# A two-layer encoder in one kernel: the projection by seven products in another order, a fourth raw weight buffer, two input sums on another engine, and both entries rearranged

## The reference

```
hn  = RMSNorm(h)
qkv = hn @ w_qkv                      (1024 x 2304)
h  += concat(attention A, attention B) @ w_o
h  += ConvGatedMLP(RMSNorm(h))        (1024 -> 5632 -> conv, SiLU gate -> 1024)
h  += (p[i] @ w_ple_proj) * sigmoid(RMSNorm(h) @ w_ple_gate)
```

## Time and profile before

| what | value |
|---|---|
| time, median of 3 runs | 2502.76 us (2502.4 to 2505.92) |
| the profiled execution's own time | 2506.71 us |
| its span | 2504.9 us |
| mean granted clock of TensorE | 0.992 |
| TensorE busy | 2433.6 us, 97% |
| VectorE busy | 1521.4 us, 61% |
| ScalarE busy | 1293.0 us, 52% |
| GpSimd busy | 1212.2 us, 48% |
| DMA, mean | 105 GB/s |

### The profile page before, as it was taken

How to read it: one execution, slowest core, us unless ns; L and a number is a source line. 1 busy time by engine, 2 the same in 40 slices (tenths; PEclk the granted TensorE clock), 3 DMA queues, 4 the chain that set the end, 5 groups by cost and what they waited for, 6 DMA issues and landing times.

```text
span 2504.9 us, 36613 instructions
## 1 busy us (share of the span) xinstructions
PE 2433.6 (97%) x12704; PEld 2116.9 (85%) x12704; DVE 1521.4 (61%) x2114; ACT 1293.0 (52%) x2020; POOL 1212.2 (48%) x881
## 2 busy tenths in 40 slices
PE   7998999999999999999989999999999999999999
PEld 6998998878888888888889889988788888888887
DVE  3587664276656668873255866733856656778733
ACT  5445774375555554444364467734655655533342
POOL 4877641148878860001339775412578888400011
PEclk9999999999999999999989999999999999999999
DMA  6642010313233248431226410103143233473312
GB/s 221 176 130 74 20 30 26 118 51 109 86 119 109 80 170 297 134 110 43 77 72 181 132 55 25 29 26 126 35 125 109 80 120 115 173 277 120 98 49 84
DMA packets 214060, 263.54 MB, mean 105 GB/s; under 512 B 17648, under 2 KB 145056, under 8 KB 213936
## 3 DMA queue, kind: packets, MB, share of 16 engines
q1 hardware_dynamic: 213376, 259.50, 32.9%
q0 software_dynamic: 560, 2.41, 0.3%
HBM read 206.83 MB, written 55.36 MB: 105 GB/s over the span
## 4 chain that ended last, share of the span: by engine, by line
PE 77%; DVE 7%; issue 6%; POOL 4%; ACT 4%; DMA 1%; SPq 0%; ACTq 0%; POOLq 0%; DVEq 0%
PE ps L3031 9%; PE ps L3034 9%; PE ps L3033 9%; PE ps L2554 7%; PE ps L2556 7%; PE ps L2555 7%; PE ps L3055 6%; PE ps L3056 6%; PE ps L3057 5%; PE ps L2807 3%; POOL w_hl L1051 2%; PE ps L2796 2%; PE ps L2725 1%; PE ps L2768 1%; PE ps L2900 1%
## 5 line engine op out<-in xcount | busy, mean ns | idle before, releaser
L1026 POOL TENSOR_TENSOR w_hl<-w_raw,w_hl 128x1024 fp32r<-128x1024 f32 x36 | 86.1, 2393 | 763.3 <-ACT w_hl L1247 763.3
L2554 PE MATMUL ps<-w_hl,xv 128*128 128x384 f32 x672 | 233.2, 347 | 28.7 <-POOL w_hl L1051 16.2
L2555 PE MATMUL ps<-w_hl,xv 128*128 128x384 f32 x672 | 228.8, 341 | 0.0
L2556 PE MATMUL ps<-w_hl,xv 128*128 128x384 f32 x672 | 228.6, 340 | 0.0
L2554 PE MATMUL ps<-w_hl,xT 128*128 128x512 f32 x512 | 202.0, 394 | 1.4 <-DVE xT L1900 0.7
L2556 PE MATMUL ps<-w_hl,xT 128*128 128x512 f32 x512 | 199.6, 390 | 0.0
L2555 PE MATMUL ps<-w_hl,xT 128*128 128x512 f32 x512 | 199.3, 389 | 0.0
L2384 DVE SCALAR_TENSOR_TENSOR ps<-c_up,ccols,ps 128x1023 f32<-128x1023 f32 x84 | 107.8, 1284 | 142.4 <-ACT ps L1679 142.4
L2363 DVE TENSOR_TENSOR c_up<-ps,kept 128x512 f32<-128x512 f32 x126 | 86.6, 689 | 125.2 <-ACT kept L1638 69.5
L2554 PEld LDWEIGHTS ps<-w_hl,xv 128*128 128x128 f32 x672 | 129.3, 192 | 36.1 <-POOL w_hl L1051 22.0
L3055 PE MATMUL ps<-bd_two,ad 128*128 128x512 f32 x392 | 152.5, 389 | 0.0
(11 more groups left out here) (322 smaller groups left out, 7309.8 us busy)
## 6 DMA issues: line engine op xcount, KB each, us to landing
ad_raw<-v_rows SPq DMA_DIRECT2D x70, 512.0 KB, 3.7
raw_a<-in_w_up SPq DMA_DIRECT2D x44, 512.0 KB, 5.0
raw_g<-in_w_up SPq DMA_DIRECT2D x44, 512.0 KB, 5.2
v_rows<-c_up SPq DMA_DIRECT2D x22, 1024.0 KB, 4.4
w_raw<-in_w_qkv SPq DMA_DIRECT2D x56, 384.0 KB, 3.3
w_raw_b<-in_w_qkv SPq DMA_DIRECT2D x48, 384.0 KB, 3.6
wd_main<-in_w_down SPq DMA_DIRECT2D x30, 512.0 KB, 8.2
v_rows<-hc_g SPq DMA_DIRECT2D x22, 512.0 KB, 5.0
```

The lines of the kernel that those rows point to most:

```text
L2554: nc.tensor.matmul(dst, lhs[:, k, 0, cols], wh, start=first, stop=False)
L2555: nc.tensor.matmul(dst, lhs[:, k, 0, cols], wl, start=False, stop=False)
L2556: return nc.tensor.matmul(dst, lhs[:, k, 1, cols], wh, start=False, stop=last)
```

## The change

The order of the products becomes 3, 5, 1, 4, 2, 7, 6. The ring of raw blocks gets a fourth buffer, `w_raw_d`, in the part of `w_hl`'s memory that the projection does not use; the projection's weights in `w_hl` are therefore packed. The two input sums on GpSimd are those of product 7 (i = 10 and 11, behind slots 26 and 30) and no longer of product 6; the weight sum for slot 32 stands behind the low part of slot 31. VectorE makes the low part of an input at m%3 = 0 between the second and the third add. At the entry ScalarE squares five token tiles and VectorE three; the high part of slot 3 stands ahead of the root, that of slot 4 between the first writes of the two output blocks; in layer 0 the first weight load stands ahead of the rows, and the loads of slots 2 to 6 ahead of the constants; waits for the constants move out of the entry. In layer 1 two of the first four slices are transposed behind rows 4 and 5 of the gate's last part, and their high and low parts stand behind the gate's last two tiles on ScalarE and VectorE. The bias set-up on GpSimd moves behind slots 7, 8, 9 and 11. At attention's entry the fills come one row earlier, the copies of the second head pair no longer wait for the second part of the head norms, and the four high parts stand ahead of the second root.

```diff
-Q_ORDER = (3, 5, 7, 4, 1, 2, 6)
+Q_ORDER = (3, 5, 1, 4, 2, 7, 6)
-Q_FINAL = {5: "C12", 1: "C11", 2: "C21", 6: "C22"}
+Q_FINAL = {5: "C12", 2: "C21", 7: "C11", 6: "C22"}
+Q_POOL = (10, 11)
+Q_LEAD = 2
-ENTRY_FILLS = {1: (0, 1), 2: (2,), 3: (3,)}
+ENTRY_FILLS = {0: (0, 1), 1: (2,), 2: (3,)}
+ONE_RING = 4
+SQUARED_FIRST = 5
...
         def one_raw(slot):
-            return w_raw_c[:, :] if slot % 3 == 2 else w_raw[:, slot % 3, 0:2 * QC]
+            at = slot % ONE_RING
+            if at == 3:
+                return w_raw_d[:, :, 4 * QC:5 * QC]
+            return (w_raw_c[:, :] if at == 2 else w_raw[:, at, 0:2 * QC]).rearrange("p (k n) -> p k n", k=2)
...
-                sp.wait_ge(s_w_low_ready, L * SLOTS + (slot + 1 if slot < 2 else slot))
+                if slot < 2:
+                    sp.wait_ge(s_w_low_ready, L * SLOTS + slot + 1)
+                elif slot == 3:
+                    sp.wait_ge(s_w_used, L * SLOTS + C_USED)
+                elif slot > 3:
+                    sp.wait_ge(s_w_low_ready, L * SLOTS + slot - 1)
...
+            load_qkv(0, 0)
             for j in range(TT // 2):
                 sp.dma_start(h[:, 2 * j:2 * j + 2, :], x_rows[:, 2 * j:2 * j + 2, :]).then_inc(h_loaded[j], 16)
-                if j < 2:
-                    load_qkv(0, j)
+                if j == 1:
+                    load_qkv(0, 1)
+            for slot in range(2, 7):
+                load_qkv(0, slot)
...
-                between = {1: set_consts, 2: negate_bias, 3: store_bias, 4: skew_bias} if L == 0 else {}
+                between = {7: set_consts, 8: negate_bias, 9: store_bias, 11: skew_bias} if L == 0 else {}
...
-                    if slot in (O0 - 10, O0 - 6):
-                        input_sum(12 if slot == O0 - 10 else 13)
-                    if slot + 2 < O0:
-                        qkv_sum(slot + 2)
+                    if slot == 26:
+                        input_sum(Q_POOL[0])
+                    if slot == 30:
+                        input_sum(Q_POOL[1])
+                        continue
+                    if slot == 31:
+                        qkv_sum(30 + Q_LEAD)
+                    if slot + Q_LEAD < O0:
+                        qkv_sum(slot + Q_LEAD)
...
                     pool.wait_ge(s_fill_ready, L * FILLS + (4 * hd + C_FILL - 4))
-                    if hd == 1:
-                        pool.wait_ge(s_q_rstd_ready, L * 2 + 2)
...
                     copies(hd)
-                    if hd == 0:
+                    if hd == 1:
                         low(O0)
+                        pool.wait_ge(s_q_rstd_ready, L * 2 + 2)
...
-                for m in range(4):
-                    first_high(m)
+                for m in range(2 if L else 0, 4):
+                    first_high(L, m)
...
                 first_keep(12)
+                square_tile(3)
                 first_keep(14)
-                square_tile(3)
+                square_tile(4)
                 if L:
                     table(ACT.Sqrt)
+                qkv_high(L, 3)
                 norm_root(0)
-                act.wait_ge(s_consts_loaded, CONSTS)
-                act.wait_ge(s_consts_set, 1)
...
                     for name, sign in Q_FIRST.get(q_product(m), ()):
+                        if m == 0 and name == "C22":
+                            qkv_high(L, 4)
...
-                entry_high(0)
-                entry_high(1)
+                act.wait_ge(s_consts_set, 1)
+                for f in range(4):
+                    entry_high(f)
                 act.wait_ge(s_q_mean_ready, L * 2 + 2)
                 nc.scalar.activation(q_rstd[:, :, 24:], q_sum[:, :, 24:], ACT.Sqrt).then_inc(s_q_rms_ready, 1)
-                entry_high(2)
-                entry_high(3)
...
+                        if n and t >= 6 and L < DEPTH - 1:
+                            first_high(L + 1, t - 6)
...
-                first_low(0)
-                first_low(1)
-                first_low(2)
-                first_low(3)
+                for m in range(2 if L else 0, 4):
+                    first_low(L, m)
                 first_keep(1)
                 first_keep(3)
+                square_tile(5)
                 first_keep(5)
                 first_keep(7)
-                square_tile(4)
+                square_tile(6)
                 first_keep(9)
-                square_tile(5)
                 first_keep(11)
-                square_tile(6)
+                square_tile(7)
                 first_keep(13)
-                square_tile(7)
                 first_keep(15)
...
-                    step_adds(m - 1)
-                    i = 2 * (m // 3 + 1)
-                    made = i < 14 and Q_ORDER[i // 2] in Q_INPUTS and Q_ORDER[i // 2] != 6
-                    if m % 3 == 0 and m > 1:
+                    if m % 3 == 0:
+                        step_adds(m - 1, (0, 1))
                         input_low(2 * (m // 3) + 1)
+                        step_adds(m - 1, (2, 3))
+                    else:
+                        step_adds(m - 1)
...
-                dve.wait_ge(s_w_used, L * SLOTS + (O0 - 1 + C_USED))
+                dve.wait_ge(s_w_sum, L * Q_TWO + Q_TWO)
                 for b in range(2):
                     nc.vector.memset(bias[0:HD, b, WIN_B - HD:WIN_B], BIG)
...
+                        if n and t >= 6 and L < DEPTH - 1:
+                            first_low(L + 1, t - 6)
...
+                    else:
+                        pe.wait_ge(s_gate_sig, L * 2 * TT - TT + 4)
+                        first_slice(L, 2)
+                        first_slice(L, 3)
...
+                        def next_slice(t):
+                            if t in (4, 5) and L < DEPTH - 1:
+                                pe.wait_ge(s_gate_sig, L * 2 * TT + (TT + t - 4 + 1))
+                                pe.wait_ge(s_gate_added, L * 2 * TT + (TT + C_GATE))
+                                first_slice(L + 1, t - 4)
```

More of the change, by code:

```diff
@@ L142, in q_squares, with one_bytes @@
     return 4 * sum(q_normed(x) for x in range(m))
+def one_bytes(L, s):
+    per = RAW_DMAS if s % ONE_RING < 2 else 16 * len(range(s % ONE_RING, O0, ONE_RING))
+    return L * per + 16 * (s // ONE_RING + 1)
 def q_twos(s):
@@ L157, in input_sums, with ring_free @@
 def input_sums(i):
-    return sum(Q_ORDER[x // 2] in Q_INPUTS and Q_ORDER[x // 2] != 6 for x in range(i))
+    return sum(Q_ORDER[x // 2] in Q_INPUTS and x not in Q_POOL for x in range(2, i))
+def ring_free(i):
+    return 6 * ((i - 3) // 2) + 4 + (i - 3) % 2 + 1
 def products_of(u):
@@ L318, in trunk @@
         r0 = ExitStack()
+        w_raw_d = sb("w_raw_d", [P, 2, 2048], F, r0)
+        r0.close()
+        r0 = ExitStack()
         bd_two = sb("bd_two", [P, 2, 2, 2, HALF], R, r0)
@@ L837, in tiled @@
                     return src.rearrange("a (k p) n -> p (a k) n", p=P)
-                for slot in range(0 if L else 2, O0):
+                for slot in range(0 if L else 7, O0):
                     load_qkv(L, slot)
@@ L2008, in step_adds @@
                         dve.wait_ge(s_q_copied, L * Q_COPIES + q_copies(m - 2))
-                    for t in range(4 if targets else 0):
+                    for t in tiles if targets else ():
                         q_add(m, 0, t)
@@ L2037, in _ @@
                         step_rest(m - 1)
[L2038 removed]
+                    if made and m % 3 == 2:
+                        input_sum(i)
+                    if i and m % 3 == 1:
                         input_low(i)
[L2040 to L2041 removed]
                     if m == QSTEPS - 2:
@@ L2544, in _, with first_slice @@
             pe.wait_ge(s_first_loaded, 32)
+            def first_slice(L, m, tiles=range(4)):
+                k, half = BY_TOKENS[m]
+                for t in tiles:
+                    last = nc.tensor.transpose(first_bank(m)[:, t * P:(t + 1) * P],
+                                               h[:, 4 * half + t, k * P:(k + 1) * P], ident[:, :])
+                if tiles[-1] == 3:
+                    last.then_inc(s_xfill, 1)
             for L in range(DEPTH):
```

199 lines of the change are left out of this document (101 added, 98 removed).

## The result

| | before | changed |
|---|---|---|
| median of 20 runs each, side by side | 2504.76 us | 2498.18 us |
| lowest to highest | 2500.61 to 2507.14 | 2495.42 to 2504.21 |
| ratio to before, 95% interval | | 0.9976 (0.9969 to 0.9982) |
| profiled execution, own time | 2506.71 us | 2496.61 us |
| its span | 2504.9 us | 2494.8 us |

The change is a gain, but a third of the one forecast (2484, range 2473 to 2497), and the time lies above the range. The two profiles differ by 10.1 us and not by 6.6: the one of before lies high among its runs, the one of the changed kernel low. I use them for where time went, stretch by stretch, and the medians for how much.

What follows compares the result with a forecast made beforehand. TensorE, busy 97% of the span, was taken as the bound, so only its waits and low clock could be won. Terms -5.9 - 4.1 - 4.2 - 2.6 - 1.8 - 1.3 + 0.8 = -19.1 from 2506.7, less 3.95: 2484 us, range 2473 to 2497.

Steps and rivals of the forecast that it cites:

- Entry: Slots 2 to 5: earlier high parts shrink stalls and low clock, gaining 5.9 us in layer 0, 4.1 in layer 1.
- The lock: Port pair shared by VectorE and GpSimd: held exclusively for a whole instruction, so delays are whole instructions.
- Layer 1's slot 3: Entry of layer 1: stall shrinks from 3.07 to about 1.6 us, with no fall of the clock.
- The skew transfer: Slots 10 to 13, layer 0: the transfer moved to slot 11 delays a weight load, +0.8 us, bounds 0 and +5.
- Slots 24 and 25: VectorE's low part no longer beside a GpSimd sum and behind two adds, not four: -4.2 and -2.6 us.
- Slots 30 to 37: Products with most adds parted, product 7's input sums on GpSimd: -0.9 us each layer, -1.8 together.
- Attention's entry: Second `k_nat` no longer waits for the second root: -0.4 and -0.85 us, together -1.3, bounds -5.3 and +2.7.
- d: Attention's entry: delay of VectorE's work before the first scores, beside GpSimd's earlier copies; taken as 2 us, from 0 to 4.
- Start of the projections: Start of both layers' projections: zero change; bound -1.9 us in layer 1.
- Given back: Rival, 0.20: clock falls at layer 1's entry, port delays attention's entry by 4 each layer, slots 30 to 37 unchanged; 2492.6 us.
- GpSimd becomes the bound: Rival, 0.05: steps with two weight blocks slow when VectorE blocks GpSimd operations, 1.1 us over in each of 24; 2510 us.
- signs of being wrong: TensorE stall above 2 us for GpSimd in slots 12-23 or 34-41, late raw load near slot 13, entry excess above 3 us.

Runs made afterwards that it cites:

- Experiment 4: Changed kernel, but GpSimd's weight sum for slot 5 waits until VectorE has refined the norm factors; 2493.25 us, ratio 0.9955.
- experiment 5: Changed kernel with bias set-up behind slots 4 to 7, sinks' copies moved, entry reordered on ScalarE and GpSimd, layer 1's table load earlier; 2480.31 us, 0.9912.
- experiment 7: Changed kernel, but VectorE's low part of an input at the third step stands behind all four adds, as before; 2503.4 us, 0.9996.
- experiment 1: Changed kernel, but bias set-up with its skew transfer behind slots 4, 5, 6, 7 of layer 0, not 7, 8, 9, 11; 2492.9 us, 0.9952.
- experiment 3: Changed kernel, but ScalarE makes the high part of slot 4 right behind the root, not between the output blocks' writes; 2500.6 us, 0.9984.
- experiment 8: Changed kernel, but VectorE makes product 7's two input sums and GpSimd none; 2497.35 us, 0.9972.
- experiment 9: Changed kernel, but GpSimd's second-head-pair copies wait for the second head norms again, slot O0's low part ahead of them; 2500.5 us, 0.9982.
- experiment 6: Changed kernel with a ring of three raw buffers, as before, instead of four; 2501.1 us, 0.9986.

## Why the prediction was wrong, point by point

**Entry, the step that failed.** I let "the root's ScalarE work then run beside slot 3" and gave VectorE's refinement no price, so I had low(4) "done about when slot 3 ends: 0.3" late. It was 3.0 late, and in both profiled layers the low clock added 1.7. The lock was priced elsewhere in the same text, from the same rows. I had applied it to the long operations (a low part, a mean) and not to the tiny ones of 0.17 us that make the factors. By the move of low(3) they came under GpSimd, and two were caught in each layer. Price missed: 4.0 + 4.2 us. Experiment 4 takes back 3.0 in each layer by the order of GpSimd alone, experiment 5 3.9 and 4.7. Layer 1's slot 3 behaved as forecast: it began 1.6 us late, at full clock.

**The skew transfer, mis-sized and in part missed.** The term was +0.8, bound +5; it measured +5.5. The row I used, 7.9 us, was a load beside the transfer among slots of one weight block. Beside it with two blocks a slot the loads took 11.7 and 12.3, so 8.4 to 9.0 late and not 4.6, against the 4 of slack that I had. By the trace that size alone puts slot 14 where it began. The 3.3 us in front of slot 13 are another step, which the prediction did not have: it let VectorE's work there "stay as they are", and its input sum took 6.64 us and not 2.26.

**Slots 24 and 25: right,** in size in both layers, and by both causes named: about two thirds the GpSimd sum that is gone, one third the adds (experiment 7).

**Slots 30 to 37: +0.1 for -1.8.** I named the two stalls at slots 31 and 32 with 1.4 each; they measured 1.3 and 1.3. The small waits behind them, which I had at 0.2, were 1.7 in layer 0 (2.3 in experiments 1, 3 and 4) and 1.4 in layer 1. The waits are for GpSimd's low parts, and GpSimd is busy 34.2 us of 37.5; that it has no idle time to catch up in fits, but experiment 8, with as little of it, has smaller waits. So the slots rather lost up to 0.9 in layer 0 and gained 0.1 in layer 1.

**Attention's entry: d about right, the gain behind it larger.** The first scores came 1.67 us later against slot 41 than before in layer 0 (9.07 for 7.40) and 3.2 later in layer 1 (9.08 for 5.86), and 2.1 in each by experiment 9; d was taken as 2. The copies that met the port were the sinks', as said. The stretch behind slot 41 fell by 2.4 and 2.0 in the profiles, 1.7 and 1.8 by experiment 9, where I had 0.4 and 0.9. The low clock there was shorter too, 6.8 and 3.4 us for 10.2 in each layer before, which I had not counted; part of it is scatter, since layer 1 had 3.4 or 6.8 in profiles of the same code.

**Start of the projections.** Zero was forecast, -1.5 and -1.2 came. Neither is shown as a gain. With the same code the stretch had 6.7 to 8.1 us of excess in layer 0 and 5.4 to 7.7 in layer 1 in the runs above; the kernel before had 8.2 and 8.1. In layer 1 it goes with the low clock over slot 0, 3.4 us in the changed kernel, 6.8 before and again in experiment 6.

**The rivals.** "Given back" had the right idea (port, clock, slots 30 to 37) and the wrong place for the largest part. "GpSimd becomes the bound" did not come: slots 15 to 22, with two weight blocks each, still took 4.16 each; only slots 30 to 37 show some of it. Two of the signs of being wrong did show: more than 3 us of excess at both entries, and a raw load that ends the wait of slot 14.

What stays open: 3.5 us between the profiles' difference and the medians', 1.95 of it since the profiled run of the kernel before lies above its median. Profiles of kernels with the same code there differ by up to 1.5 us at the start of layer 0, by 1.7 where the clock falls or holds behind the same gap at slot 4, by 1.3 in slots 30 to 37 of layer 0, and by 1 to 2 us behind slot 41. The new order of products was not tried by itself, nor the long sum of VectorE under the transfer.

## What to carry to other kernels

When work of GpSimd is moved, list every VectorE operation that will run beside it, down to those of 8 columns: one that took 0.17 us can take 1.8, and each link of a chain on the way to a factor is a chance. Place GpSimd's work by a wait behind such a chain (or the chain into a gap of GpSimd's), and put a large transfer where the loads beside it are fewest. A moved transfer must be priced by the loads of its new place. Where the profile names an engine for a wait on two semaphores, look when the exact operation that was needed had ended.

## What the runs showed of the hardware that I had not expected

An operation of VectorE on 64x4 elements or 128x8 stands as long behind a GpSimd operation as one on 128x1024 (2.85 for 1.22 in the earlier trace rows): 1.6 to 1.9 us for 0.15 to 0.17. The Trainium skill's "SBUF — State Buffer", section "SBUF: two separate sides", counts among those that take the lock a VectorE operation with two SBUF inputs or in a 2-port mode; the trace agrees for the two-input ones, and a COPY and a TENSOR_SCALAR with one input were caught too, whose mode no view here shows. Not each one was caught. In the changed kernel the COPY at 213.82 and the TENSOR_SCALAR at 217.57, which began as one GpSimd instruction gave way to the next, took 0.15 and 0.16. And the kind decides: the RECIPROCAL of 128x8 took 0.20 inside GpSimd's low(3) as it does alone, and the adds from PSUM (SCALAR_TENSOR_TENSOR) took 0.60 to 0.62 in all 192 cases, 173 of them begun while GpSimd worked.

One operation of VectorE can stand behind more than one of GpSimd's: the input sum of slot 13 took 6.64 us and ended behind the third, while its like in layer 1 stood behind one (2.26).

The granted clock did not follow the length of a gap alone. Behind the same gap at slot 4 (TensorE idle 2.7 us) it fell in both layers of the changed kernel, and held in layer 0 of experiments 1 and 8 and in layer 1 of experiment 9: 3 of the 14 such gaps in the profiles of this code.
